# Encoder layer with expert choice: prompt rows of four experts in one gather, start loads issued without waits, low parts moved around the first gather

## What is computed

```
mod = silu(c) @ w_ada + b_ada ; shift1, scale1, gate1, shift2, scale2, gate2 = split(mod)
h = RMSNorm(x) * (1 + scale1) + shift1
[qA|kA|vA|qB|kB|vB|gA|gB] = h @ w_in
x = x + gate1 * ((sigmoid(gA) * global_attn(..) @ w_a + sigmoid(gB) * window_attn(..) @ w_b) @ w_out)
h2 = RMSNorm(x) * (1 + scale2) + shift2
for each of 16 experts: the top 2n/16 tokens of each group by softmax(h2 @ w_router)
    y = (silu(h2[idx] @ w_gate) * (h2[idx] @ w_up)) @ w_down * g ; scatter-add to the tokens
x = x + gate2 * y ; y = RMSNorm(x)
```

## Time and profile before

| what | us |
|---|---|
| median of 3 runs | 2379.2 (2378.38 to 2379.95) |
| the profiled execution | 2382.7 |
| span of its trace | 2380.6 |
| DVE, ACT, POOL busy in it | 1644.9, 1217.2, 1114.4 |

### The profile page before, as it was taken

How to read it: one execution, slowest core, us unless ns; L and a number is a source line. 1 busy time by engine, 2 the same in 40 slices (tenths; PEclk the granted TensorE clock), 3 DMA queues, 4 the chain that set the end, 5 groups by cost and what they waited for, 6 DMA issues and landing times.

```text
span 2380.6 us, 54919 instructions
## 1 busy us (share of the span) xinstructions
PE 2320.5 (97%) x23918; PEld 1689.0 (71%) x23918; DVE 1644.9 (69%) x2053; ACT 1217.2 (51%) x1542; POOL 1114.4 (47%) x703
## 2 busy tenths in 40 slices
PE   8999999999999999979999999999999999999996
PEld 3554676665444457768888888888888888888874
DVE  4765565475222455868787888798788878887875
ACT  4323555575111235445556656555655565556554
POOL 0000111123332314657576677677567766766642
PEclk9999999999999999979999999999999999999998
DMA  9102101502112355568899899989999998999896
GB/s 339 37 18 75 50 1 37 178 2 79 43 48 54 98 168 154 167 228 309 318 326 323 310 335 329 321 317 321 338 313 336 323 327 313 332 329 321 316 328 245
DMA packets 252583, 524.09 MB, mean 220 GB/s; under 512 B 8588, under 2 KB 57853, under 8 KB 252221
## 3 DMA queue, kind: packets, MB, share of 16 engines
q1 hardware_dynamic: 241692, 488.51, 58.4%
q0 software_dynamic: 10656, 32.12, 4.7%
HBM read 492.29 MB, written 28.31 MB: 219 GB/s over the span
## 4 chain that ended last, share of the span: by engine, by line
PE 92%; DVE 3%; DMA 2%; ACT 1%; issue 1%; SPq 1%; POOL 0%; DVEq 0%; POOLq 0%; ACTq 0%
PE ps L1757 24%; PE ps L1758 23%; PE ps L1759 23%; PE ps L1934 4%; PE ps L1946 4%; PE ps L2135 4%; PE ps L1915 3%; PE ps L1925 1%; DVE arena L1593 1%; PE ps L2081 1%; PE ps L1834 1%; PE ps L1786 1%; DMA arena<-w_in 1%; PE ps L1955 1%; PE ps L1872 1%
## 5 line engine op out<-in xcount | busy, mean ns | idle before, releaser
L1757 PE MATMUL ps<-arena 128*128 128x160 bf16 (+4 forms) x5624 | 1394.6, 267 | 3.0 <-DVE arena L1642 2.7
L1759 PE MATMUL ps<-arena 128*128 128x160 bf16 (+4 forms) x5624 | 1394.6, 267 | 0.9 <-issue 0.9
L1758 PE MATMUL ps<-arena 128*128 128x160 bf16 (+4 forms) x5624 | 1394.7, 267 | 0.0
L1593 DVE TENSOR_TENSOR arena<-arena 128x2048 bf16<-128x2048 f32 x379 | 931.2, 2461 | 179.5 <-ACT arena L936 179.0
L936 ACT ACTIVATE arena<-arena 128x2048 bf16<-128x2048 f32 x384 | 726.7, 1904 | 219.4 <-PE ps L1759 179.1
L1757 PEld LDWEIGHTS ps<-arena 128*128 128x128 bf16 x5624 | 551.0, 98 | 155.4 <-issue 14.0
L1759 PEld LDWEIGHTS ps<-arena 128*128 128x128 bf16 x5624 | 551.0, 98 | 153.3 <-issue 1.1
L1758 PEld LDWEIGHTS ps<-arena 128*128 128x128 bf16 x5624 | 551.1, 98 | 140.1 <-issue 0.3
L846 POOL TENSOR_TENSOR arena<-arena 128x320 bf16<-128x320 f32 x128 | 275.5, 2152 | 10.0
L843 POOL TENSOR_TENSOR arena<-arena,ones 128x320 bf16<-128x320 f32 x128 | 194.6, 1520 | 140.6 <-DVE arena L1642 140.4
L1183 ACT ACTIVATE arena<-ps 128x160 f32<-128x160 f32 x256 | 77.5, 303 | 319.6 <-PE ps L1759 319.6
(11 more groups left out here) (256 smaller groups left out, 2226.4 us busy)
## 6 DMA issues: line engine op xcount, KB each, us to landing
arena<-w_e_gate SPq DMA_DIRECT2D x64, 2048.0 KB, 8.9
arena<-w_e_up SPq DMA_DIRECT2D x64, 2048.0 KB, 9.6
arena<-w_e_down SPq DMA_DIRECT2D x64, 2048.0 KB, 9.0
arena<-w_ada SPq DMA_DIRECT2D x12, 2048.0 KB, 9.1
arena<-w_in SPq DMA_DIRECT2D x30, 512.0 KB, 5.2
arena<-x_sample SPq DMA_DIRECT2D x16, 512.0 KB, 3.6
arena<-w_in SPq DMA_DIRECT2D x3, 2048.0 KB, 16.2
arena<-w_out SPq DMA_DIRECT2D x2, 2048.0 KB, 9.5
```

The source lines that it names most:

```text
L1593: ve.tensor_tensor(lo, stage_half(kind, a), hi, ALU.subtract).then_inc(lo_done, 1)
L1757: pe.matmul(out, w_hi, x_hi, start=start, stop=False)
L1758: pe.matmul(out, w_hi, x_lo, start=False, stop=False)
L1759: return pe.matmul(out, w_lo, x_hi, start=False, stop=stop)
```

## The change

Three parts.

Rows of four experts: a gather of prompt rows takes 128 rows, 32 for each of four experts, at experts 0, 3, 7 and 11 (`fours`); the very first gather stays one of 32 rows for expert 0. PE transposes the 128 rows in eight transposes behind feature blocks 12 and 13 (`group_turned`), DVE modulates them in eight instructions (`modulate_group`) into `xpT`, which lies over the gathered rows, and POOL splits one expert's 32 columns per expert behind hidden pair 6 (`split_prompt_rows`). The indices of four experts are laid out by four DVE instructions in the first expert (`group_indices`), behind product 1. The three groups of transposes per expert keep the sample rows alone. PE waits for `xp_ready` at the head of each expert from the second on.

Loads: w_ada chunks 0 to 2 get places of their own beside w_in's, so the three w_in loads are issued behind w_ada without a wait, and the load of x tile 1 behind them; the waits for AR move to ACT's split of w_in, whose high parts lie over w_ada.

Low parts: DVE makes low part 5 when POOL has issued the first gather (`ye_free`), and parts 6 and 7 behind the split of the gathered rows.

More of the change, by code:

```diff
@@ L441, in encoder @@
         xe_mod = sem("xe_mod")
+        gi_ready, xp_done, xp_mod, xp_high, xp_ready = [sem(n) for n in ("gi_ready", "xp_done", "xp_mod", "xp_high", "xp_ready")]
         nf_in = sem("nf_in")
@@ L744, in gather_rows, with gather_first @@
                                       in_offset=bass.IndirectOffsetOnAxis(ap=gidx[b][:, 0:1], axis=0)).then_inc(gat[b], 16)
-            def gather():
-                gather_rows(1)
-                gather_rows(0)
+            def gather_first():
+                gp.indirect_dma_start(out=xeP[0:CAP_P], out_offset=None, in_=xn_d[0],
+                                      in_offset=bass.IndirectOffsetOnAxis(ap=gidx[0][0:CAP_P, 0:1], axis=0)).then_inc(gat[0], 16)
             def low_first(h):
@@ L831, in split_rows @@
                 gp.wait_ge(xe_mod, mods + n + 1)
-                gp.tensor_tensor(xeT[par][:, 0, d0:d1], src,
-                                 ones[:, 0:d1 - d0].unsqueeze(2).to_broadcast([P, d1 - d0, SLOTS]), ALU.mult).then_inc(high, 1)
+                dst = xeT[par][:, :, d0:d1, 0:CAP_S]
+                gp.tensor_tensor(dst[:, 0], src,
+                                 ones[:, 0:d1 - d0].unsqueeze(2).to_broadcast([P, d1 - d0, CAP_S]), ALU.mult).then_inc(high, 1)
                 gp.wait_ge(high, highs)
-                gp.tensor_tensor(xeT[par][:, 1, d0:d1], src, xeT[par][:, 0, d0:d1], ALU.subtract)\
-                    .then_inc(xe_ready, 1)
+                gp.tensor_tensor(dst[:, 1], src, dst[:, 0], ALU.subtract).then_inc(xe_ready, 1)
+            def split_prompt_rows(e, par):
[6 more added lines that the diff above has]
+                gp.tensor_tensor(dst[:, 1], src, dst[:, 0], ALU.subtract).then_inc(xp_ready, 1)
             def split_hidden(e, p, highs, par):
@@ L869, in _, with copies @@
             gp.wait_ge(idx_ready, 5)
-            gp.tensor_copy(gidx[0][:], idx[0][:, 0:1]).then_inc(cidx, 1)
+            gp.tensor_copy(gidx[0][0:CAP_P], idx[0][:, 0:1]).then_inc(cidx, 1)
             gp.wait_ge(cidx, 2)
-            gather_rows(0)
+            gather_first()
             gp.tensor_tensor(spare[:, 2:3], ones[:, 0:1], ones[:, 1:2], ALU.add).then_inc(ye_free, 1)
+            def copies(e):
+                return 2 + e + 1 + gathered(e) + 2 * max(e - 1, 0)
             def expert_pool(e, par, first=False, last=False):
@@ L889, in expert_pool @@
                     if last and p == 6:
-                        scatter(e - 1, 4 * e)
+                        scatter(e - 1, copies(e - 1) + 2)
                     split_hidden(e, p, h0 + n, par)
@@ L893, in expert_pool @@
                         split_rows(3 * e + 3, h0 + n + 1, p - 3, 1 - par)
+                    if p == 6 and not last:
+                        split_prompt_rows(e + 1, 1 - par)
                 if not first and not last:
-                    scatter(e - 1, 4 * e + 2)
+                    scatter(e - 1, copies(e))
             expert_pool(0, 0, first=True)
@@ L906, in _ @@
             gp.tensor_copy(sidx[1][:], idx[1][:, NE - 1:NE]).then_inc(cidx, 1)
-            gp.wait_ge(cidx, 4 * NE)
+            gp.wait_ge(cidx, copies(NE - 2) + 6)
             gp.wait_ge(xe_done, 3 * NE)
@@ L1647, in expert_vec @@
                         product(f)
+                        if f == 1:
+                            group_indices()
                         splits(f)
@@ L1650, in expert_vec @@
                             modulate_rows(3, (f - 7) // 2, 1)
+                        if f in (12, 13):
+                            modulate_group(e, f - 12)
                 else:
@@ L1662, in expert_vec @@
                             modulate_rows(3 * e + 3, (s - 11) // 2, 1 - par)
+                        if s in (18, 19) and e in fours:
+                            modulate_group(e, s - 18)
                     if kind != "last":
@@ L2106, in xe_transposes @@
                 for d in range(d0, d1):
[L2107 to L2112 removed]
+                    o = (d - d0) * CAP_S
+                    ins = pe.transpose(ps[:, 6 + n % 2, o:o + CAP_S], xeS[:, d * P:(d + 1) * P], ident[:])
+                ins.then_inc(xe_done, 1)
+            def group_turned(e, n):
[5 more added lines that the diff above has]
+                ins.then_inc(xp_done, 1)
             pe.wait_ge(idx_ready, 5)
@@ L2116, in _ @@
             for d in range(KD):
-                ins = pe.transpose(ps[:, 6, d * CAP_P:(d + 1) * CAP_P], xeP[:, d * P:(d + 1) * P], ident[0:CAP_P, 0:CAP_P])
+                ins = pe.transpose(ps[:, 6, d * CAP_P:(d + 1) * CAP_P], xeP[0:CAP_P, d * P:(d + 1) * P],
+                                   ident[0:CAP_P, 0:CAP_P])
             ins.then_inc(xe_done, 3)
```

14 lines of the change are left out of this document (7 added, 7 removed).

## The result

| | us |
|---|---|
| before, median of 5 runs | 2379.2 (2378.38 to 2380.44) |
| after, median of 5 runs | 2390.77 (2388.97 to 2391.07) |
| ratio after to before, 95% interval | 1.0042 [1.003, 1.0053] |
| after, profiled execution / its span | 2390.83 / 2389.0 |

The change makes the kernel slower by 0.42%.

The account below looks back on a forecast made before the run. TensorE, busy 97% of the span, was taken to bound the kernel. Terms -7.5 + 0.5 + 24.2 - 5.4 = +11.8 gave 2391.0 us against a median of 2379.2, range 2381 to 2398.

Parts of the forecast that it names:

- part 1, transposes: Experts: 120 narrow transposes removed at 0.10 us, 32 wide added at 0.14; -7.5 us, ends -10.3 and -6.8.
- part 1, first expert: First expert: second gathers wait for DVE's index arithmetic, and the first hidden pair's split queues behind; +0.5 us, ends 0 and 4.
- part 2: Start: late x tile 1 holds ScalarE's copy of the modulation row, then DVE is late; +24.2 us, ends 19.7 and 26.7.
- part 3: Hand-over to the first expert: index copy and gather issue no longer held by DVE; -5.4 us, ends -7 and -1.
- Rival 3: Whole kernel: the forecast itself, 2391 us, own range 2386 to 2397; chance 0.66.
- The low clock: Start: PE at half clock after standing over 20 us, until about AR 3; +4.5 us, ends 0 and 7.
- Rival 1: Start: PE at its high clock at once, start costs 19.7 us, total 2386.5, or 2382.1 at best ends; chance 0.10.
- rival 2: Start: tile 1 lands early, no hold-up, and the hole is closed; -3.4 us there, total 2363.4; chance 0.09.
- What counts is start to start: Experts: transposes priced by spacing of record starts, 0.10 us narrow and 0.14 wide, since records overlap.
- Cost of the new wait for `xp_ready` in the first expert: Head of the next expert: POOL's prompt split finishes before PE needs it; priced at 0.
- the -24.2 by that figure: Experts: alternative estimate of part 1, 88 fewer transposes at the skill's 275 ns each; -24.2 us, set aside for the trace's spacing.
- Rival 4: First expert: held copies and gathers make sample rows or product 4 late, up to +4 us, low-clock start; 2397.0; chance 0.15.

Follow-up runs that it names:

- order: Kernel after, x tile 1 still loaded last, with ScalarE's square of tile 1 (XP 1) moved behind X 0 in the step list; 2379.06 us, ratio 0.999.
- x1_first: Kernel after with the load of x tile 1 back ahead of w_ada, the w_in loads still early; 2365.59 us, ratio 0.9936.
- part1: Kernel before with the rows of four experts alone, loads and low parts as before; 2372.94 us, ratio 0.9971.
- gi_early: Kernel after with DVE's index arithmetic for the second gathers moved ahead of low part 5; 2389.98 us, ratio 1.0041.
- group_early: x1_first with index arithmetic ahead of low part 5, first expert's group transposes at blocks 4 and 5, prompt split behind pair 2; 2358.7 us, ratio 0.9906.
- p1_group_early: Kernel before with rows of four, index arithmetic ahead of low parts 5 and 6, first expert's group at blocks 4 and 5; 2360.15 us, ratio 0.9919.
- closed: p1_group_early with the three w_in loads early and x tile 1 still ahead of w_ada; 2356.23 us, ratio 0.9899.

## Why the prediction was right, and where its terms were not

| term | predicted | measured |
|---|---|---|
| part 1, transposes | -7.5 | -13.5 in the steady experts (112 narrow less at 0.145, 24 wide more at 0.12) |
| part 1, first expert | +0.5 | +9.5 in after, 7.3 to 7.5 in order and x1_first; +6.3 in part1 |
| part 2 | +24.2 | +22.6 at the start of G 2; +21.7 to idx; +23.0 alone |
| part 3 | -5.4 | -7.3 at product 0; -5.2 alone |
| sum | +11.8 | +10.4 by the marks, +11.6 by the medians |

Rival 3 came out, at its centre, and that it did so to 0.2 us is luck: the two terms of part 1 were wrong by 6 and by 7 to 9 us in opposite senses, and those of parts 2 and 3 were too high by some 2 each. What wasn't luck is the sign and the bulk of it, part 2.

**Part 2, right in mechanism and nearly in size.** Square of tile 1 predicted at 46.3, measured 46.38; the copy 47.8 and 47.86; G 0 64.2 and 62.37. The low clock was charged with 4.5; PE was back at its high clock by AR 3 (1.92), so 2.7 is nearer (62.4 - 59.7). DVE then came late as the forecast had it: G 1's first matmul came at 83.07, 20.3 later than in before, but G 2's at 102.81, 22.6 later (80.24 in before's timeline), and 40.4 behind G 0's start, as forecast. Rival 1, the high clock at once, is refuted by AR 2's 3.64; rival 2, no hold-up, by the wait of 22.9. Its working (2363.4) is within 2.2 of what x1_first gave when the hold-up was taken away (2365.6), with the two misses of part 1 cancelling in it too. The Trainium skill, "DMA: Bandwidth & Descriptors", Queues, rings and completion order, says that completion is not first-in first-out per issuing engine; here 0.5 MB behind 14 MB of the same queue landed last, in order.

**Part 1, the step that failed first.** "What counts is start to start", read once, in one group of three: 0.10 for a narrow one, 0.14 for a wide one. The 0.72 for three and three was right, its split between the two was not: a wide transpose next to narrow ones is itself slower (0.14 to 0.16) than without them (0.11 to 0.13), and per narrow one the group of two cost more than the one read ((0.55 - 0.22) / 2 = 0.165). I had rejected the merged busy time of 0.123 per narrow one as too high; even it was too low. The Trainium skill, "TensorE: Matmul & The Clock Gate", Part 4, gives some 275 ns: a record of L2161 is 272 to 330 ns long in the trace, but among other work one costs 0.11 to 0.13, so that neither the -24.2 by that figure nor my -7.5 came out.

**Part 1, the step that failed second.** Cost of the new wait for `xp_ready` in the first expert: I argued that it "ends when POOL has split them behind the seventh hidden pair, before the eighth, so ahead of the next expert", and priced it at 0, with the room of 12 us per expert from the earlier trace rows, a window of the steady experts, where it holds. The first expert has no down products, and DVE (93% busy) and POOL (85%) have little of that room there; PE stood for 6.2 us. Rival 4 named the first expert, but with the wrong mechanism (held gathers; gi_early refutes it) and half the price. And no case had the clock in the price of a wait there: one of 4 to 6 us on PE cost 1.7 to 2.8 more behind it.

**Part 3, mechanism right, size small by 2.** Copy and issue took 0.18 and 0.92 as predicted. The gather landed 2.9 us behind the issue's start, not 4.4 (from 1059.23 on, in the chain of after). And PE stood for 1.4, not 2.5 us, and stayed at its high clock: 1.00 from 1062.3 to 1066, where before it had 0.50 from 1047.8 to 1052, behind its wait of 8.6. That is the upper end that the forecast gave. Some of it is lost later: alone, part 3 gave 5.2.

## What to carry to other kernels

When a load is moved, look not only for who needs its data but for which engine's list has that step, and what stands behind it there: `order` took back about 12 us of the loss without touching the load. Price a new wait in the stage with the least room, not in the steady one, and add the low clock behind it: 1.7 to 2.8 us here behind waits of 4 to 6 us, and in some cases 1.7 behind one of 2 to 3. A cost per instruction read from one group is a guess; put the instructions back into the final kernel, without their effect, and divide.

## What the runs showed of the hardware

- **The clock behind a wait of PE.** In all 14 traces every wait of 3.8 us or more, except the one of some 5 us that opens the span, was followed by a granted 0.50, 1.2 GHz instead of 2.4: 4.1 (group_early), 5.1 (part1), 6.2 and 23.1 (after) by 3.4 to 6 us of it. Waits of 1.9 to 3.2 us went either way. Behind 2.5 and 2.9 us the clock stayed whole in after; behind 2.0 us in x1_first (until 1088.47) and 2.7 in before (until 1104.43) it fell to 0.50 for 3.4 us:
```profile
1090.00:1093.00 3.00, 3.00 (x25) 3.00 (x24) 3.00 (x7) 0.00 (x0) 2.92 (x3) 0.50 1.01 387
1105.30:1108.50 3.20, 3.20 (x26) 3.20 (x25) 3.20 (x2) 1.24 (x1) 3.20 (x2) 0.50 1.05 405
```
  p1_group_early even has 3.4 us at 0.50 from 1048.1 on, with no wait over 1.4 us in the 20 us before it. So the length of a wait alone doesn't decide; what does is left open.
- **SP is held by its own queue.** With seven loads of 2 MB in a row the last three took 5.5 us each to issue, about what one needs to land behind another (5.3), and one of 0.5 MB behind them took as long (SP's timeline, after):
```profile
14.18 16.57 SPq L584 DMA_DIRECT2D arena<-w_in  x3
30.80 5.29 SPq L585 DMA_DIRECT2D arena<-x_prompt  x1
```
  In the kernel before a load into an idle queue was issued in 0.37 (w_in chunk 0, at 23.58).
- **POOL beside DVE.** An index copy takes 0.17 to 0.19 us and an indirect DMA's issue 0.90 to 1.04 beside nothing or beside DVE's light index arithmetic and modulations. Started while a low part is under way, the copy ends with it (0.8 to 2.3) and the issue 0.8 to 0.9 behind it (2.0 to 2.9). Started together with the low part (closed, 1033.98) the issue takes 0.92 and isn't held. The Trainium skill, "GPSIMD Engine Reference", 1. Specifications, has POOL's SBUF interfaces shared with VectorE, with contention from instructions with two SBUF inputs; a low part is one, the index arithmetic isn't, and these numbers agree, but for the issue that started with the low part.
- **Transposes side by side.** 0.11 to 0.13 us for one of 128 rows among matmuls, 0.14 to 0.145 for one of 32 rows behind them, its effect on its neighbours included: the smaller one is the dearer.
